# The low-rank norms of the attention's inputs, computed inside the input projection; the convolution's layer norm, inside the attention's projections

## The chip, the cores and the metric

The kernel is one program on one core of a Trainium2 chip. It runs two layers of a sequence mixer with an MLP behind each, and then one layer of another kind; all inputs and sums are float32. The metric is the device time of one execution in microseconds. The kernel before was timed in three runs, 3916.98 to 3918.47 us, with a median of 3918.4 us.

## The reference

There are 512 tokens of x and 256 of context, 768 together, each with 1024 features. What follows is the mixer of a layer, cut to what the change touches. In layer 0 all of it is computed for both kinds of token. In layer 1 the context takes part as keys, values and memory alone (`with_ctx` is false), so its convolution and its queries are not needed.

```python
DEPTH = 2;  CONV_DIM = 512;  CONV_K = 31;  Q_LORA = 768;  KV_LORA = 256;  QK_ROPE = 32

def layer_norm(x, g, b):
    mu = jnp.mean(x, -1, keepdims=True)
    var = jnp.mean(jnp.square(x - mu), -1, keepdims=True)
    return (x - mu) * lax.rsqrt(var + LN_EPS) * g + b

def rms_norm(x, g):
    return x * lax.rsqrt(jnp.mean(jnp.square(x), -1, keepdims=True) + LN_EPS) * g

def conformer_conv(a, w_dw, b_dw, g, b, w_pw):
    val, gate = jnp.split(a, 2, axis=-1)
    h = val * jax.nn.sigmoid(gate)
    h = depthwise_conv(h, w_dw, taps=CONV_K) + b_dw        # along the tokens, 15 before to 15 behind
    return jax.nn.silu(layer_norm(h, g, b)) @ w_pw

def mla_project(cq, ckv, kr, qn_g, w_uq, kvn_g, w_ukv, rope):
    q = rms_norm(cq, qn_g) @ w_uq                          # 8 heads of 64 + 32
    kv = rms_norm(ckv, kvn_g) @ w_ukv                      # 8 heads of 64 + 64
    ...                                                    # the 32s of q, and kr, are rotated

def token_mixer(u, uc, ...):
    a, qkv, o_pre, g_if, cq, ckv, kr, gates = jnp.split(u @ w_in + b_in, IN_SPLITS, axis=-1)
    y_conv = conformer_conv(a, ...)
    y_ml = mlstm_out(...)                                  # from qkv, o_pre, g_if
    o_x = attention over mla_project(cq, ckv, kr, ...)
    return gated_merge(gates, y_conv, y_ml, o_x @ w_mla_out, w_out, b_out)
```

## The kernel before, in words

Activations lie transposed: features on the 128 partitions, tokens along the free axis, 768 wide (512 and 256 for the two token kinds; 512 alone where layer 1 leaves the context out). A norm over features is therefore a sum over partitions. TensorE makes it with a matrix of ones, which also spreads the sum over all partitions.

**Weights.** They stream from HBM in groups of 128 output columns through a ring of 4 slots (`weight_ring`, queue of SP). The first three functions below that name runs and groups count a group as one slot. `plan_weights` fixes the order of the groups; in `project_stage` it is conv 8, qkv 12, o 4, cq 6, ckv 2, small 1: 33 groups in each layer. A group of such a product is split into a high part, made by ACT (L365, two groups ahead), and a low part, the subtraction on GpSimd (L373, `weights_low<-weight_ring,weights_high`).

**A group on TensorE** (`product`, L431): 8 feature tiles times the column parts, first the high weights by the high and the low activations (L448, L449), then, after a wait for the split, the low weights by the high activations (L454, 16 passes for a width of 768). Groups use two PSUM tiles in turn. A group waits (`tile_free`) until the tile's previous group has been taken out.

**The convolution.** Its input comes from pairs of groups: gates in the even ones, ACT makes their sigmoid; values in the odd ones, the vector engine multiplies them (L885, called the gating here, one instruction for each token kind) and then frees the odd tile. Four gatings stand first in the vector engine's program. Behind them come the four filters, each for 128 features: one instruction of tap 0 (L898) and a loop over the 30 other taps (L900 to L904), each tap a multiply-add over 512 tokens and one over 256, in layer 1 over 512 alone.

**The norm stage** (`norm_stage`, L984) stands between the projection and the attention, with a barrier of all engines on each side. It does the convolution's layer norm with its SiLU, and the two root-mean-square norms of ckv (2 tiles) and cq (6 tiles). Its sums are plain ones: L1008 for the mean, L1018 for the squares.

**The attention's beginning** (`attention_stage`, L1114). TensorE rotates the key's rope part (L1206), projects two rope tiles of the queries and four others (`queries_of`, L1198, 6 passes of 512 columns and in layer 0 6 of 256; here called the rope products and the query products 0 to 3), turns the rope tiles (L1211), then makes four products of keys (L1233, key products 0 to 3), and then the scores (L1249). These products read the normed cq and ckv. The convolution's result is not read before a later stage.

## Time and profile before

| | |
|---|---|
| median of 3 runs (lowest, highest) | 3918.4 us (3916.98, 3918.47) |
| the profiled execution: its own time | 3919.24 us |
| its span in the profile | 3917.4 us |
| TensorE matmul busy (PE) | 3503.9 us, 89% of the span |
| TensorE weight load (PEld) | 2727.3 us, 70% |
| vector engine (DVE) | 1735.0 us, 44% |
| ACT | 1088.0 us, 28% |
| GpSimd (POOL) | 1065.1 us, 27% |
| mean granted clock of TensorE | 0.929 of full speed |
| read from HBM | 265.56 MB |

The span is the time from the first to the last instruction of the core in one profiled execution; the execution's own time is a little longer. Busy time counts the time in which an engine works on an instruction; waits, branches and register instructions are not in it. The weight load runs beside the matmuls. The full speed of the clock column is 2.4 GHz. Such means cover the whole program; what a stage is worth has to be read in the stage itself.

### The profile page before, as it was taken

What the parts mean: (1) busy time and instruction counts of PE and PEld (TensorE: products, weight loads), DVE (VectorE), ACT (ScalarE), POOL (GpSimd) and SP (SyncE); (2) the same over time, 40 slices, a digit from 0 to 9 for tenths busy, and PEclk for the clock granted to TensorE, in tenths of its full rate; (3) what the DMA queues carried; (4) which work ended last, traced back from release to release, by engine and by line L of the source; (5) the groups of instructions that cost most, each with busy time, mean ns of one, the idle gap of its engine ahead of it and who ended that gap; (6) DMA issues with size and microseconds to landing.
All of it is one profiled execution on the core that took longest, in us unless ns stands there. A gap on an engine that the chain in (4) does not pass through costs nothing. (4 is left out here: it accounts for less than half of the span.)

```text
span 3917.4 us, 48973 instructions
## 1 busy us (share of the span) xinstructions
PE 3503.9 (89%) x18326; PEld 2727.3 (70%) x18326; DVE 1735.0 (44%) x2340; ACT 1088.0 (28%) x1540; POOL 1065.1 (27%) x491
## 2 busy tenths in 40 slices
PE   5899798879998799999797997799799979899998
PEld 4787466757776688888585566566577757678786
DVE  3592445450113522323486455412433348577625
ACT  1122243121112512221423231212432245333223
POOL 2532100111112222222333001222344423344442
PEclk7999898779999899999899997799899989899998
DMA  5222133012221122222122221232133322123232
GB/s 161 54 60 53 30 102 103 24 51 56 59 59 54 34 63 61 62 64 59 55 71 52 62 65 44 70 86 82 58 92 91 92 69 68 51 86 96 83 94 75
DMA packets 549094, 269.63 MB, mean 69 GB/s; under 512 B 55922, under 2 KB 547146, under 8 KB 548827
## 3 DMA queue, kind: packets, MB, share of 16 engines
q1 hardware_dynamic: 547330, 267.26, 24.2%
q8 instruction: 93, 1.52, 0.2%
q10 hardware_dynamic: 889, 0.30, 0.0%
q14 instruction: 46, 0.38, 0.0%
q0 software_dynamic: 736, 0.17, 0.0%
HBM read 265.56 MB, written 2.10 MB: 68 GB/s over the span
## 5 line engine op out<-in xcount | busy, mean ns | idle before, releaser
L373 POOL TENSOR_TENSOR weights_low<-weight_ring,weights_high 128x1024 fp32r<-128x1024 f32 x360 | 924.3, 2569 | 1782.8 <-ACT weights_high L365 1742.2
L365 ACT ACTIVATE weights_high<-weight_ring 128x1024 fp32r<-128x1024 f32 x360 | 380.3, 1059 | 1616.0 <-PE ps L454 1169.5
L448 PE MATMUL ps<-u_high,weights_high 128*128 128x512 f32 (+2 forms) x1440 | 533.2, 380 | 42.9 <-DVE u_low L751 35.1
L449 PE MATMUL ps<-u_low,weights_high 128*128 128x512 f32 (+2 forms) x1440 | 522.1, 373 | 0.0
L448 PEld LDWEIGHTS ps<-u_high,weights_high 128*128 128x128 f32 (+1 forms) x1440 | 275.8, 191 | 105.6 <-issue 29.6
L454 PE MATMUL ps<-u_high,weights_low 128*128 128x512 f32 (+2 forms) x1440 | 319.2, 369 | 15.8 <-POOL weights_low L373 15.8
L449 PEld LDWEIGHTS ps<-u_low,weights_high 128*128 128x128 f32 (+1 forms) x1440 | 276.9, 192 | 51.0 <-issue 3.7
L448 PE MATMUL ps<-mlp_u_high,weights_high 128*128 128x512 f32 (+1 forms) x768 | 268.4, 363 | 43.3 <-DVE mlp_u_low L751 42.3
L904 DVE SCALAR_TENSOR_TENSOR arena<-arena,vectors 128x512 f32<-128x512 f32 x360 | 293.2, 864 | 30.3 <-DVE arena L904 29.3
L454 PEld LDWEIGHTS ps<-u_high,weights_low 128*128 128x128 f32 (+1 forms) x1440 | 249.7, 190 | 61.6 <-POOL weights_low L373 16.0
L448 PE MATMUL ps<-hidden_high,weights_high 128*128 128x512 f32 (+1 forms) x768 | 263.8, 357 | 15.4 <-DVE hidden_low L2107 15.4
L449 PE MATMUL ps<-mlp_u_low,weights_high 128*128 128x512 f32 (+1 forms) x768 | 265.1, 360 | 0.0
L449 PE MATMUL ps<-hidden_low,weights_high 128*128 128x512 f32 (+1 forms) x768 | 261.5, 356 | 0.0
L2105 DVE TENSOR_TENSOR mlp_work<-mlp_work 128x768 f32<-128x768 f32 (+1 forms) x64 | 152.4, 2381 | 224.6 <-ACT mlp_work L2085 224.6
L1929 DVE TENSOR_TENSOR arena<-ps,arena 128x768 f32<-128x768 f32 (+3 forms) x48 | 39.6, 824 | 463.1 <-PE ps L467 463.1
L448 PE MATMUL ps<-merge_u_high,weights_high 128*128 128x512 f32 x576 | 212.0, 380 | 21.9 <-DVE merge_u_low L751 21.5
L2116 DVE SCALAR_TENSOR_TENSOR x_features<-ps,modulation,x_features 128x512 f32<-128x512 f32 x96 | 60.6, 659 | 355.0 <-PE ps L454 355.0
L467 PE MATMUL ps<-arena,weight_ring 128*128 128x512 f32 (+1 forms) x576 | 210.1, 521 | 0.0
L449 PE MATMUL ps<-merge_u_low,weights_high 128*128 128x512 f32 x576 | 201.8, 364 | 0.0
L448 PEld LDWEIGHTS ps<-mlp_u_high,weights_high 128*128 128x128 f32 x768 | 146.6, 191 | 72.9 <-issue 32.6
L448 PEld LDWEIGHTS ps<-hidden_high,weights_high 128*128 128x128 f32 x768 | 144.6, 188 | 40.5 <-DVE hidden_low L2107 17.9
L467 PEld LDWEIGHTS ps<-arena,weight_ring 128*128 128x128 f32 x576 | 108.5, 190 | 92.1 <-issue 86.1
(470 smaller groups left out, 5611.4 us busy)
## 6 DMA issues: line engine op xcount, KB each, us to landing
weight_ring<-in_w_in SPq DMA_DIRECT2D x262, 256.0 KB, 3.2
weight_ring<-in_w SPq DMA_DIRECT2D x256, 256.0 KB, 3.1
weight_ring<-in_w_mod SPq DMA_DIRECT2D x192, 256.0 KB, 4.0
weight_ring<-in_w_up SPq DMA_DIRECT2D x88, 256.0 KB, 3.1
weight_ring<-in_w_out SPq DMA_DIRECT2D x48, 256.0 KB, 3.1
weight_ring<-in_w_down SPq DMA_DIRECT2D x32, 256.0 KB, 3.2
weight_ring<-in_w_conv_out SPq DMA_DIRECT2D x32, 128.0 KB, 2.3
weight_ring<-in_w_mlstm_out SPq DMA_DIRECT2D x32, 128.0 KB, 2.3
```

Of the source, the lines that this page charges most:

```text
L365: act.activation(core.ring_high[:, split_slot(run, q), :], core.ring[:, slot, :], ACT.Copy).then_inc(core.high_ready.sem, 1)
L373: core.nc.gpsimd.tensor_tensor(core.ring_low[:, split_slot(run, q), :], core.ring[:, (run.first + q) % SLOTS, :], high.bitcast(F32), ALU.s ...
L448: pe.matmul(out[:, a:b], w_high[:, k, 0:m], high(k, a, b), start=(first and k == 0), stop=False, skip_group_check=True)
L449: pe.matmul(out[:, a:b], w_high[:, k, 0:m], low(k, a, b), start=False, stop=False, skip_group_check=True)
L454: mm = pe.matmul(out[:, a:b], w_low[:, k, 0:m], high(k, a, b), start=False, stop=(last and k == kts - 1), skip_group_check=True)
L467: mm = pe.matmul(out[:, a:b], w[:, k, :], rhs(k, a, b), start=(k == 0), stop=(k == kts - 1))
L904: nc.vector.scalar_tensor_tensor(conv[:, f, a:b], pads[:, f, bass.ds(t + at, b - a)], w_dw[:, bass.ds(t, 1), f], conv[:, f, a:b], ALU.mult ...
L1929: nc.vector.tensor_tensor(dst, gemm(core, 2 + f, w), sig[:, f, 0:w], ALU.mult).then_inc(multiplied.sem, 1)
L2105: nc.vector.tensor_tensor(squares[:, q % 2, 0:w], tmp[:, q % 2, 0:w], tmp[:, q % 2, 0:w], ALU.mult).then_inc(made.sem, 1)
L2116: ins = nc.vector.scalar_tensor_tensor(x, gemm(core, q % 2)[:, a:b], core.mod[l][:, 40 + q, j:j + 1], x, ALU.mult, ALU.add)
```

## The change

The groups of the projection are reordered: cq, ckv and small come right behind conv, and qkv and o behind these. The squares of cq and ckv are made by ACT as their groups come out, into room that qkv will fill later. TensorE sums them in a form of its own, `spread_sums`: four tiles at a time, each by a matrix of ones 32 columns wide, into its own 32 partitions of the output (behind cq's fifth group, and behind small). ACT copies the result, and `total_of_spread` (behind qkv's second group) adds up the four parts and spreads the total over all partitions. ACT makes the first guess of the reciprocal root (a logarithm, an exponential) behind qkv's third group. The vector engine refines it and scales cq and ckv (`scale_low_rank`, 16 instructions) between filters 2 and 3. ACT waits for that before qkv's ninth group, whose output lies where the intermediate values are.

On the vector engine filter 0 is cut into three loops of 10 taps, and the gatings 1 to 3 stand behind them.

The convolution's layer norm moves into the attention's projections. TensorE sums its four tiles before the first rope product, totals them behind it, and does the same for the squares behind query product 0 and query product 1. ACT makes the copies, squares, logarithm, exponential and the four SiLUs; the vector engine centers, refines and scales. Key product 0 now waits for the halved variance (`step` 2), since it takes the total's PSUM tile. ACT waits for the scaling before it copies the first keys, and GpSimd before its copies of the key's rope part. PSUM tiles are dealt out anew. The norm stage is no longer called. The diff, cut to what is spoken of:

```diff
         add(f"conv{l}", 8, paired(w_in, OFF_CONV + CONV_DIM, OFF_CONV))
-        add(f"qkv{l}", 12, plain(w_in, OFF_QKV))
-        add(f"o{l}", 4, plain(w_in, OFF_O))
         add(f"cq{l}", 6, plain(w_in, OFF_CQ))
...
         add(f"small{l}", 1, small)
+        add(f"qkv{l}", 12, plain(w_in, OFF_QKV))
+        add(f"o{l}", 4, plain(w_in, OFF_O))
...
+def spread_sums(core, pe, out, tiles, first, last):
...
+    for a, b in parts(T):
+        for g, tile in tiles:
+            if b <= tile.shape[1]:
+                mm = pe.matmul(out(g)[g * 32:(g + 1) * 32, a:b], core.ones[:, 0:32], tile[:, a:b], start=first(g), stop=last(g),
+                               skip_group_check=True)
+    return mm
...
+def total_of_spread(core, pe, out, partial, rows):
...
+    for a, b in parts(partial.shape[1]):
+        mm = pe.matmul(out[:, a:b], core.ones[rows, :], partial[rows, a:b], start=True, stop=True)
...
+                if (name, g) == ("cq", 4):
+                    pe.wait_ge(squared.sem, squared.at(4))
+                    spread_sums(core, pe, lambda j: gemm(core, 2), [(j, squares[:, j, 0:wx]) for j in range(4)], lambda j: True,
+                                lambda j: j >= 2).then_inc(half_summed.sem, 1)
+                elif name == "small":
+                    pe.wait_ge(squared.sem, squared.at(8))
+                    spread_sums(core, pe, lambda j: gemm(core, 2 + j // 2), [(j, squares[:, j, 0:(wx, T)[j // 2]]) for j in range(4)],
+                                lambda j: j >= 2, lambda j: True).then_inc(spread_summed.sem, 1)
+                elif (name, g) == ("qkv", 1):
+                    pe.wait_ge(spread_copied.sem, spread_copied.at(2))
+                    for j, (_, _, w, _, rows) in enumerate(norms):
+                        mm = total_of_spread(core, pe, gemm(core, 2 + j), partial[:, j, 0:w], rows)
+                    mm.then_inc(totals_ready.sem, 1)
...
                 elif name == "qkv":
+                    if g == 8:
+                        act.wait_ge(scaled.sem, scaled.at(8))
...
+                    if g >= 4:
+                        act.wait_ge(half_summed.sem, half_summed.at(1))
+                    act.activation(squares[:, g % 4, 0:w], src, ACT.Square, bias=col(core, f"b_cq{l}", g)).then_inc(squared.sem, 1)
                     act.activation(cq[:, g, 0:w], src, ACT.Identity, bias=col(core, f"b_cq{l}", g)).then_inc(free[f].sem, 1)
...
+                    act.activation(squares[:, 2 + g, 0:w], src, ACT.Square, bias=col(core, f"b_ckv{l}", g)).then_inc(squared.sem, 1)
...
+                elif (name, g) == ("qkv", 2):
+                    act.wait_ge(totals_ready.sem, totals_ready.at(1))
+                    for j, (_, tiles, w, _, _) in enumerate(norms):
+                        act.activation(rstd[:, j, 0:w], gemm(core, 2 + j, w), ACT.Ln, scale=1.0 / (32 * tiles * P),
+                                       bias=core.eps[:, 0:1]).then_inc(logged.sem, 1)
+                    for j, (_, _, w, _, _) in enumerate(norms):
+                        act.wait_ge(logged.sem, logged.at(j + 1))
+                        act.activation(rstd[:, j, 0:w], rstd[:, j, 0:w], ACT.Exp, scale=-0.5).then_inc(rstd_step.sem, 1)
...
-            for q in range(4):
+            def conv_input(q):
...
+            def scale_low_rank():
+                dve.wait_ge(rstd_step.sem, rstd_step.at(2))
+                for j, (_, tiles, w, _, _) in enumerate(norms):
...
+                for j, (z, tiles, w, gain, _) in enumerate(norms):
+                    dve.wait_ge(rstd_step.sem, rstd_step.at(9 + j))
+                    for k in range(tiles):
+                        nc.vector.scalar_tensor_tensor(z[:, k, 0:w], z[:, k, 0:w], col(core, gain, k), rstd[:, j, 0:w], ALU.mult,
+                                                       ALU.mult).then_inc(scaled.sem, 1)
...
+            def taps(f, lo, hi):
+                with dve.Fori(lo, hi) as t:
+                    for j, (a, b, at) in enumerate(spans):
...
+            conv_input(0)
             for f in range(4):
                 if f:
...
+                if f == 0:
+                    for q in range(1, 4):
+                        taps(0, 10 * q - 9, 10 * q + 1)
+                        conv_input(q)
+                else:
+                    taps(f, 1, CONV_K)
+                if f == 2:
+                    scale_low_rank()
...
+            def conv_sums(tiles):
+                spread_sums(core, pe, lambda g: gemm(core, 3), list(enumerate(tiles)), lambda g: True, lambda g: True)\
+                    .then_inc(c["spread_summed"].sem, 1)
+            def conv_totals(n):
+                pe.wait_ge(c["copied"].sem, c["copied"].at(n))
+                total_of_spread(core, pe, gemm(core, 3), partial[:, 0:wz], slice(0, P)).then_inc(c["totals_ready"].sem, 1)
+            conv_sums([z[:, f, 0:wz] for f in range(4)])
             pe.wait_ge(core.rope_weights.sem, core.rope_weights.at(64))
             queries_of("rope", 0, "qr0")
+            conv_totals(1)
             queries_of("rope", 1, "qr1")
             turn_queries(0)
+            pe.wait_ge(s["kr_rotated"].sem, s["kr_rotated"].at(1))
             queries_of("nope", 0, "qn0")
+            pe.wait_ge(c["squared"].sem, c["squared"].at(4))
+            conv_sums([squares[f][:, 0:wz] for f in range(4)])
...
+            pe.wait_ge(s["rope_step"].sem, s["rope_step"].at(1))
             queries_of("nope", 1, "qn1")
-            pe.wait_ge(s["rope_step"].sem, s["rope_step"].at(1))
+            conv_totals(2)
...
             queries_of("nope", 2, "qn2")
-            pe.wait_ge(s["rope_step"].sem, s["rope_step"].at(3))
+            pe.wait_ge(s["even_copied"].sem, s["even_copied"].at(1))
+            pe.wait_ge(s["odd_copied"].sem, s["odd_copied"].at(1))
             queries_of("nope", 3, "qn3")
...
+                if p:
+                    pe.wait_ge(s["even_copied"].sem, s["even_copied"].at(p + 3))
+                    pe.wait_ge(s["odd_copied"].sem, s["odd_copied"].at(p + 3))
+                else:
+                    pe.wait_ge(c["step"].sem, c["step"].at(2))
...
+                act.wait_ge(c["spread_summed"].sem, c["spread_summed"].at(n))
+                act.activation(partial[:, 0:wz], conv_total, ACT.Copy).then_inc(c["copied"].sem, 1)
+            spread_copy(1)
             raw_queries(0)
+            for f in range(4):
+                act.wait_ge(c["centered"].sem, c["centered"].at(f + 1))
+                act.activation(squares[f][:, 0:wz], z[:, f, 0:wz], ACT.Square).then_inc(c["squared"].sem, 1)
             raw_queries(1)
             for p in range(PAIRS):
+                if p == 1:
+                    spread_copy(2)
+                elif p == 2:
+                    act.wait_ge(c["totals_ready"].sem, c["totals_ready"].at(2))
+                    act.activation(mean[:, 0:wz], conv_total, ACT.Ln, scale=1.0 / (32 * CONV_DIM), bias=core.eps[:, 0:1])\
+                        .then_inc(c["logged"].sem, 1)
+                    act.wait_ge(c["logged"].sem, c["logged"].at(1))
+                    act.activation(mean[:, 0:wz], mean[:, 0:wz], ACT.Exp, scale=-0.5).then_inc(c["step"].sem, 1)
+                elif p == 3:
+                    for f in range(4):
+                        act.wait_ge(c["scaled"].sem, c["scaled"].at(f + 1))
+                        act.activation(z[:, f, 0:wz], z[:, f, 0:wz], ACT.Silu, scale=col(core, f"cn_g{l}", f), bias=col(core, f"cn_b{l}", f))
                 projected(act, f"qn{p}")
...
+                if p == 0:
+                    act.wait_ge(c["scaled"].sem, c["scaled"].at(4))
...
+            pool.wait_ge(c["scaled"].sem, c["scaled"].at(4))
...
+            dve.wait_ge(c["totals_ready"].sem, c["totals_ready"].at(1))
+            for f in range(4):
+                nc.vector.scalar_tensor_tensor(z[:, f, 0:wz], conv_total, -1.0 / (32 * CONV_DIM), z[:, f, 0:wz], ALU.mult,
...
+            step = c["step"]
+            dve.wait_ge(step.sem, step.at(1))
+            nc.vector.tensor_scalar(half[:, 0:wz], conv_total, -0.5 / (32 * CONV_DIM), -0.5 * LN_EPS, ALU.mult, ALU.add).then_inc(step.sem, 1)
...
-                    norm_stage(core, *norms)
                     attention_stage(core, l)
```

The tables of the program's order show two places. Names in capitals are instructions, ISA is a short one that carries a wait or a loop's counter, and [waits ...] names the semaphores that a row waits for.

The vector engine in layer 0, before: the last two gatings (L885), tap 0 of filter 0 (L898), and its loop.

```order
L885 SCALAR_TENSOR_TENSOR arena<-ps,vectors,arena 128x512 [waits conv_input_ready_27,gate_sigmoid_ready_26,weights_used_0]
L885 SCALAR_TENSOR_TENSOR arena<-ps,vectors,arena 128x256
L898 TENSOR_SCALAR arena<-arena,vectors 128x512 [waits conv_input_ready_27]
L898 TENSOR_SCALAR arena<-arena,vectors 128x256
L900 UNCONDITIONAL_BRANCH
L900 ISA
L904 ISA [waits conv_step_28]
L904 SCALAR_TENSOR_TENSOR arena<-arena,vectors 128x512
L904 ISA [waits conv_step_28]
L904 SCALAR_TENSOR_TENSOR arena<-arena,vectors 128x256
L900 REGISTER_ALU
L900 COMPARE_AND_BRANCH
```

The same place now: one gating (L940), tap 0 (L983), and the first ten taps (L969 to L973). The second gating follows, then the next ten, and so on.

```order
L940 SCALAR_TENSOR_TENSOR arena<-ps,vectors,arena 128x512 [waits gate_sigmoid_ready_26,weights_used_0,pads_clear_29]
L940 SCALAR_TENSOR_TENSOR arena<-ps,vectors,arena 128x256
L983 TENSOR_SCALAR arena<-arena,vectors 128x512 [waits conv_input_ready_27]
L983 TENSOR_SCALAR arena<-arena,vectors 128x256
L969 UNCONDITIONAL_BRANCH
L969 ISA
L973 ISA [waits conv_step_28]
L973 SCALAR_TENSOR_TENSOR arena<-arena,vectors 128x512
L973 ISA [waits conv_step_28]
L973 SCALAR_TENSOR_TENSOR arena<-arena,vectors 128x256
L969 REGISTER_ALU
L969 COMPARE_AND_BRANCH
```

The three gatings have moved from in front of the filter to places between its taps, and the wait for the gates' sigmoid with them. The body of the loop is the same four instructions. In filter 1 the loop's body is another one. Before:

```order
L904 ISA [waits conv_step_28]
L904 REGISTER_ALU
L904 SCALAR_TENSOR_TENSOR arena<-arena,vectors 128x512
L903 REGISTER_ALU
L904 ISA [waits conv_step_28]
L904 SCALAR_TENSOR_TENSOR arena<-arena,vectors 128x256
```

And now, the body of filter 1's loop:

```order
L973 ISA [waits conv_step_28]
L973 REGISTER_ALU
L973 SCALAR_TENSOR_TENSOR arena<-arena,vectors 128x512
L972 REGISTER_ALU
L973 ISA [waits conv_step_28]
L973 SCALAR_TENSOR_TENSOR arena<-arena,vectors 128x256
```

Both have a REGISTER_ALU between the ISA and the first tap, and one between the taps. Filter 0's loop has neither, before and now.

TensorE at the end of layer 0's norm stage, before: the last sum of squares, the barrier, the key's rotation and the first rope products.

```order
L1018 MATMUL ps<-heads,ones 128x512 [waits norm2_squared_44]
L1018 MATMUL ps<-heads,ones 128x256
L1000 UNCONDITIONAL_BRANCH
L1189 UNCONDITIONAL_BRANCH [waits barrier_Pool_Activation_PE_DVE_SP_release]
L1206 MATMUL ps<-arena,rope 32x512 [waits rope_loaded_7]
L1198 MATMUL ps<-arena,weight_ring 128x512 [waits weights_landed1,rope_weights_landed_8]
L1198 MATMUL ps<-arena,weight_ring 128x512 x5
L1198 MATMUL ps<-arena,weight_ring 128x256 x6
L1198 MATMUL ps<-arena,weight_ring 128x512 [waits weights_landed2]
```

Now, behind the projection's last low pass: the barrier, the key's rotation, the spread sum (L784, by a matrix of ones 32 columns wide), the first rope product (L1293), the total (L792), the second.

```order
L830 UNCONDITIONAL_BRANCH
L1284 UNCONDITIONAL_BRANCH [waits barrier_Pool_Activation_PE_DVE_SP_release]
L1301 MATMUL ps<-arena,rope 32x512 [waits rope_loaded_7]
L784 MATMUL ps<-arena,ones 32x512 x4
L784 MATMUL ps<-arena,ones 32x256 x4
L1293 MATMUL ps<-arena,weight_ring 128x512 [waits weights_landed1,rope_weights_landed_8]
L1293 MATMUL ps<-arena,weight_ring 128x512 x5
L1293 MATMUL ps<-arena,weight_ring 128x256 x6
L792 MATMUL ps<-heads,ones 128x512 [waits at_conv_copied_62]
L792 MATMUL ps<-heads,ones 128x256
L1293 MATMUL ps<-arena,weight_ring 128x512 [waits weights_landed2]
```

The norm stage's sums of full width are gone, and with them one of the two barriers. Between the key's rotation and the rope products stand only sums that have no wait of their own or wait for ACT's copy.

## Rows read from the trace of the kernel before

**Rows 1.** Windows of both norm stages; each engine's busy us (instructions), granted clock, DMA.
```profile
379.40:430.00 50.60, 21.14 (x64) 11.88 (x64) 27.66 (x24) 23.44 (x27) 9.23 (x4) 0.76 0.02 4
2122.00:2160.00 38.00, 14.95 (x36) 5.86 (x35) 20.73 (x24) 18.45 (x27) 7.07 (x4) 0.78 0.00 0
```

**Rows 2.** Timeline of TensorE, layer 0; start us, us, line, operation [idle before <-releaser].
```profile
374.34 2.96 PE L454 MATMUL ps<-u_high,weights_low 128*96 128x512 f32 x16
379.44 5.40 PE L1008 MATMUL ps<-arena,ones 128*128 128x512 f32 x16 [2.14 <-PEq L807]
...
430.34 1.88 PE L1206 MATMUL ps<-arena,rope 32*32 32x512 f32 x2 [26.99 <-PEq L1000]
432.15 18.07 PE L1198 MATMUL ps<-arena,weight_ring 128*128 128x512 f32 x48
```

**Rows 3.** The same of TensorE, layer 1.
```profile
2116.14 2.96 PE L454 MATMUL ps<-u_high,weights_low 128*96 128x512 f32 x16
...
2161.65 13.41 PE L1198 MATMUL ps<-arena,weight_ring 128*128 128x512 f32 x24
```

**Rows 4.** Timeline of the vector engine, layer 0's convolution.
```profile
153.24 31.83 DVE L904 SCALAR_TENSOR_TENSOR arena<-arena,vectors 128x512 f32<-128x512 f32 x60
185.10 4.83 DVE L898 TENSOR_SCALAR arena<-arena,vectors 128x512 f32<-128x512 f32 x2
189.85 42.61 DVE L904 SCALAR_TENSOR_TENSOR arena<-arena,vectors 128x512 f32<-128x512 f32 x60
```

**Rows 5.** Timeline of GpSimd, the same stretch.
```profile
158.74 28.53 POOL L373 TENSOR_TENSOR weights_low<-weight_ring,weights_high 128x1024 fp32r<-128x1024 f32 x1 [6.03 <-ACT weights_high L365]
```

**Rows 6.** Timeline of TensorE, the same stretch.
```profile
187.32 4.79 PE L454 MATMUL ps<-u_high,weights_low 128*128 128x512 f32 x16 [15.79 <-POOL weights_low L373]
```

**Rows 7.** Timeline of ACT, ends of three groups in layer 0's projection.
```profile
157.60 1.06 ACT L365 ACTIVATE weights_high<-weight_ring 128x1024 fp32r<-128x1024 f32 x1 [7.36 <-PE ps L454]
166.02 1.06 ACT L365 ACTIVATE weights_high<-weight_ring 128x1024 fp32r<-128x1024 f32 x1 [6.57 <-PE ps L454]
192.20 1.06 ACT L365 ACTIVATE weights_high<-weight_ring 128x1024 fp32r<-128x1024 f32 x1 [24.33 <-PE ps L454]
```

**Rows 8.** Timeline of the vector engine, layer 1: first gating, first filter, second filter's start.
```profile
1915.07 0.75 DVE L885 SCALAR_TENSOR_TENSOR arena<-ps,vectors,arena 128x512 f32<-128x512 f32 x1 [9.29 <-PE ps L454]
...
1949.38 0.55 DVE L898 TENSOR_SCALAR arena<-arena,vectors 128x512 f32<-128x512 f32 x1
1950.23 2.51 DVE L904 SCALAR_TENSOR_TENSOR arena<-arena,vectors 128x512 f32<-128x512 f32 x1 [0.30 <-DVE arena L898]
1953.01 0.75 DVE L904 SCALAR_TENSOR_TENSOR arena<-arena,vectors 128x512 f32<-128x512 f32 x1 [0.27 <-DVE arena L904]
...
1993.21 0.55 DVE L898 TENSOR_SCALAR arena<-arena,vectors 128x512 f32<-128x512 f32 x1
```

**Rows 9.** Timeline of ACT, layer 1, the end of group 8.
```profile
1954.11 1.06 ACT L365 ACTIVATE weights_high<-weight_ring 128x1024 fp32r<-128x1024 f32 x1 [4.51 <-PE ps L454]
```

**Rows 10.** Timeline of TensorE in an MLP stage, round a short wait.
```profile
2956.37 0.39 PE L448 MATMUL ps<-hidden_high,weights_high 128*128 128x512 f32 x1
2956.60 0.39 PE L449 MATMUL ps<-hidden_low,weights_high 128*128 128x512 f32 x1
2959.34 0.79 PE L448 MATMUL ps<-hidden_high,weights_high 128*128 128x512 f32 x1 [2.35 <-DVE hidden_low L2107]
2960.36 3.09 PE L454 MATMUL ps<-hidden_high,weights_low 128*128 128x512 f32 x8
```

**Rows 11.** Timeline of TensorE in layer 0's attention.
```profile
459.51 23.38 PE L1198 MATMUL ps<-arena,weight_ring 128*128 128x512 f32 x72
...
508.95 1.08 PE L637 MATMUL ps<-weight_ring,conditions 128*32 128x128 f32 x32
```

**Rows 12.** Timeline of ACT in layer 0's norm stage, a table load.
```profile
404.31 1.28 ACT L1042 ACT_TABLE_LOAD   x1
```

**Rows 13.** Timeline of the vector engine in layer 0's norm stage.
```profile
424.36 5.66 DVE L1086 SCALAR_TENSOR_TENSOR arena<-arena,vectors,heads 128x768 f32<-128x768 f32 x6
```

76 lines of the change are left out of this document (54 added, 22 removed).

## The prediction

> **What bounds the kernel now.** I read the two windows that hold the norm stages first, then TensorE's rows on both sides of them, then the vector and GpSimd rows of the convolution, for that loop is cut up too. In the windows [rows 1] the reader is to see that TensorE works for 21.14 of 50.60 us in layer 0's norm stage and for 14.95 of 38.00 us in layer 1's, at a granted clock of 0.76 and 0.78 of 2.4 GHz, while before and behind it is the engine that everything waits for. Its rows [rows 2, 3] give the borders: in layer 0 the last projection product ends at 374.34 + 2.96 = 377.30, the second rope product at 432.15 + 18.07 = 450.22: 72.9 us. In layer 1 the borders are 2116.14 + 2.96 = 2119.10 and 2161.65 + 13.41 = 2175.06: 56.0 us. All of this is on the path.
>
> The second place is inside layer 0's projection [rows 4 to 7]. Filter 0's 60 tap instructions run 31.83 us without a gap; the GpSimd subtraction that makes the low half of a weight group starts at 158.74 and takes 28.53 us, until the vector engine comes to filter 1's first instruction at 185.10. TensorE waits 15.79 us for it and then runs 16 low passes in 4.79 us where they take 2.96 elsewhere [rows 2]. From group to group ACT's rows are 8.42 us apart (157.60, 166.02) and here 26.18 (166.02, 192.20). So the starved subtraction costs 17.8 us. Filter 1's 60 taps take 42.61 us, and TensorE does not stall there: the subtraction gets in between. In the order of instructions filter 0's loop of layer 0 is the one without a REGISTER_ALU between its taps, before and after.
>
> **The change, part by part.**
>
> 1. *Filter 0 cut in three (layer 0).* A chunk is 20 instructions, 31.83 / 3 = 10.6 us, inside two groups, 16.8 us, with 1.3 us of gating and one wait for a subtraction of about 2.5 us (it holds up a tap that is 0.75 us long until 2.51, [rows 8]): it ends before the next odd group does, so TensorE waits for no gating. A subtraction asked for 1.1 us behind a group's end (158.74 against 157.60) is due 8.42 + 8.42 − 2.96 = 13.9 us behind that end, where the low passes after the next begin, 12.8 us after it was asked for. The worst it can meet is a whole chunk and its own length, 13.1 us. So the stall goes: −17.8. Bounds: nothing gained (it is starved as before) to −17.8.
>
> 2. *The same cut in layer 1.* Here a group lasts 5.58 us, and the gating now stands between taps. Counted from 0, group 5 cannot start before gating 1, group 7 before gating 2, group 9 before gating 3, for they use the same PSUM tile. One filter takes 1993.21 − 1949.38 = 43.8 us [rows 8]: 30 taps of 0.75 + 0.25, and 7 of them long (2.51) because a subtraction holds the vector engine up. Gating 0 is at 1915.07; behind it come 0.9 us to the filter, 43.8 us, and 3 more gatings of 1.1 us: 1963.1 before group 9 may start. In the old trace group 8 ends at 1954.1 [rows 9]. TensorE is held back 9.1 us, in three waits of about 1.5, 5 and 3 us. After a wait of 2.35 us [rows 10] ten passes run from 2959.34 to 2963.45, 4.1 us, where passes 0.23 us apart (2956.37, 2956.60) and the last one's tail take 2.5: 1.6 us lost at the lower clock. Only the last wait's loss counts, the vector engine sets the time until then: with 0.2 us for each of the waits to be seen, +1.8. Together +10.9. Bounds: 0 (if the subtractions cost the taps nothing: 7 × 1.76 = 12.3 us less) to +16 (each of the three waits with its own 1.7 us at the lower clock, and two more subtractions met).
>
> 3. *Sums in the projection.* A float32 pass of 512 columns takes 0.43 us and one of 256 takes 0.215: 72 passes in 23.38 us [rows 11]. A plain sum of four 768-wide tiles is 4 × 1.29 = 5.16 us. The new ones use 32 columns of the array for each tile. The trace has no such product 512 wide; the nearest is L637 with 128 columns, 32 passes in 1.08 us [rows 11], 0.034 each against 0.107 at the rate above: 3.2 times as fast. So a sum costs 1.6 us (between 1.29, a quarter, and 5.16, no overlap at all), in layer 1 1.1 or 1.3. Two sums in each layer: +3.2 and +2.4. Two totals: +2.6 and +2.15. What they wait for (squares, the copy) is made by ACT in the group before, where it idles over 6 of 8.4 us [rows 7]. ACT's extra work at the third qkv group (two table loads of 1.28 us [rows 12], two logarithms and two exponentials of 0.9, about 6 us) is over before its next weight part is due in either layer. The vector engine's 16 instructions for scaling, at 5.66 / 6 = 0.94 to 0.96 us [rows 13], about 16 us, stand between filters 2 and 3, and ACT waits for them only at the ninth qkv group. Counted back from the projection's end (377.3 − 17.8 + 5.8), the third qkv group has 13 groups behind it and ends near 256, so the rstd is there near 263 and the values are scaled near 285; the ninth qkv group ends near 306. In layer 1 filter 2 ends near 2053 (1963 + 2 × 45), the scaling near 2070, the ninth qkv group near 2087. The last filter ends well before TensorE does: nothing on the path.
>
> 4. *The norm stages go.* Behind the last projection product now come one barrier instead of two, about 1.4 us (2.1 before, 377.30 to 379.44, in which ACT had two evictions and now has one), the key rotation 0.9 (1.88 at the lower clock), one sum, a rope product of 7.74, a total of 1.29, a rope product of 7.74: 20.7 us in place of 72.9: −52.2. The 2.1 us gap before L1008 did not lower the clock, so I count full speed. Layer 1: 1.4 + 0.9 + 1.1 + 5.15 + 0.86 + 5.15 = 14.6 in place of 56.0: −41.4. What is late next: layer 0's weights for these products land 3 us after issue and are asked for three groups earlier.
>
> 5. *Added behind that.* One more sum and one more total: +2.9 in layer 0, +1.9 in layer 1. The new wait is that of key product 0 for the halved variance, with everything of the attention queued behind it. With t the end of query product 1: total at t + 1.3, ACT's table load, Ln, table load, Exp to t + 6, vector engine to t + 7. Key product 0 comes at t + 1.3 + 2 × 7.74 = t + 16.8 (layer 1: t + 11.2 against t + 5.8). Key product 1 also needs ACT's copy of query product 3, which now stands behind four SiLUs: t + 18 against t + 19.4, in layer 1 t + 13.6 against t + 13.8. Costed at nothing; in layer 1 a microsecond more on ACT would show at once. GpSimd's key copies now wait for the scaling, but end near t + 20.5, seven microseconds before the first score.
>
> Sum, layer 0: −17.8 + 5.8 − 52.2 + 2.9 = −61.3. Layer 1: +10.9 + 4.6 − 41.4 + 1.9 = −24.0. Together −85.3. The profiled execution took 3919.2 us (span 3917.4), so 3834; it is 0.8 us above the median of the runs, which is less than I can resolve.
>
> The Trainium skill, page "TensorEngine Tiling (Array Packing)", section "Theoretical Speedup", allows up to four times for 32 columns. With its factor, an estimate, all eight sums would cost 2.2 us less than with the 3.2 of the row, and the result would be 3832. Its section "Tiling Modes" also says that changing the tiling mode drains the engine, which speaks against sums strewn among full-width products; no row here prices that.
>
> **Rivals.**
>
> *Sums without overlap.* If four column groups 512 wide run one after the other, the eight sums cost 35.2 us instead of 11.0: 3858. For it: no wide one has been seen. Against it: L637 reads four different moving operands too.
>
> *No wait in layer 1.* If TensorE is not held by the gating, part 2 gives 0 and the time is 3823. For it: each microsecond that TensorE stands still takes subtractions away from the vector engine. Against it: with no long tap at all the chain ends 12.3 us earlier, at 1950.8 where 1954.1 is needed, so only one or two of the seven subtractions may cost it anything.
>
> *Starvation moves.* The scaling has 8 instructions without a wait between them, 7.8 us, and with those in front 14 or so; if they shut the subtraction out as filter 0 does, it comes up to 3.4 us late, with 2 us of clock, and in the chunks of filter 0 some may come late as well: up to 12 us, 3846. The Trainium skill, page "SBUF — State Buffer", section "SBUF: two separate sides", has the port between the two engines as a lock held for one whole instruction, so that the other would get in after each tap. The trace agrees for the single long tap (2.51 us) and disagrees for the 28.53 us one; by the page this rival would not exist.
>
> *Slower.* The one mechanism that reaches the other side is this starvation in all filters. If the register instruction between the taps no longer lets the subtraction in, filters 1 to 3 of layer 0 cost 17.8 us each, 53, and the four of layer 1, each some 22.5 us of taps against a reserve of 5 to 10 us, about 11 each: 45. Then 3834 + 98 = 3932. It decides from about 87 us of new stalls. Against it: those loops keep their instructions.
>
> **How the numbers follow.** Forecast 0.62; sums without overlap 0.11; no wait in layer 1 0.10; starvation moves 0.14, with anything else late in the attention; slower 0.02; and 0.01 that gains and losses cancel. The forecast case alone spans 3826 to 3843. The range reaches into the cases on both sides: 3820 to 3859. A measurement of this kernel tells about 0.2% (8 us) from no change. All cases but the last two are faster by more: 0.97; same 0.01; slower 0.02.
>
> **What would show it.** Right: no row of GpSimd's subtraction over about 14 us in layer 0; TensorE waiting near groups 5, 7 and 9 of layer 1 for the gating, 9 us together; the new 32-column sums at about 1.6 us for 16 passes; under 2 us between the last projection product and the attention's first, at the full clock; 12 passes of width 512 and 12 of 256 in 7.74 us right behind. Wrong: those sums near 5 us; a wait at key product 0 or 1; a wait of a low product for GpSimd; a lower clock at the start of the attention.

## The result and the profile after

The changed kernel takes 3831.1 us (median of 4 runs, 3829.5 to 3831.8), the one before 3917.7 us (4 runs, 3915.2 to 3918.5): a ratio of 0.9779, with a 95% interval of 0.9763 to 0.9796. That is 86.6 us less; forecast were 85.3, and 3834. All medians here are of executions at the usual clock: a single one, of the kernel with layer 0's filter 0 whole, took 4350 us at a granted clock of 0.76 and is left out.

| | before | changed |
|---|---|---|
| span of the profiled execution | 3917.4 us | 3827.6 us |
| TensorE busy | 3503.9 us, 89% | 3477.7 us, 91% |
| vector engine | 1735.0 us | 1743.1 us |
| ACT | 1088.0 us | 1099.6 us |
| GpSimd | 1065.1 us | 1036.7 us |
| mean granted clock | 0.929 | 0.938 |

Busy time hardly moved: TensorE worked 26 us less and waited 64 us less. Where it did so is read by stretches of the span. A window of the changed kernel is set from the first product of a projection to the end of its last, and from there to key product 0. The columns are the stretch and its length, busy us of TensorE, weight load, vector engine, ACT and GpSimd with their instructions, the granted clock, and the DMA. First the changed kernel, layer 0's two stretches and layer 1's:

```profile
68.09:365.61 297.52, 291.47 (x1624) 249.06 (x1624) 210.42 (x288) 80.06 (x91) 105.48 (x36) 0.97 0.22 55
365.61:421.88 56.27, 54.84 (x191) 30.64 (x192) 25.46 (x38) 19.30 (x21) 3.69 (x5) 1.00 0.22 50
1829.62:2074.32 244.70, 229.09 (x1082) 183.39 (x1082) 175.32 (x160) 74.13 (x91) 90.37 (x36) 0.95 0.26 68
2074.32:2114.97 40.65, 39.22 (x99) 16.32 (x100) 19.84 (x30) 15.20 (x21) 0.86 (x2) 0.96 0.30 68
```

Then the stretches of the kernel before (its first projection runs from 67.31 to 377.30, 309.99 us):

```profile
377.30:482.74 105.44, 73.54 (x215) 41.22 (x216) 42.20 (x50) 29.27 (x34) 15.48 (x12) 0.85 0.12 27
1889.00:2119.10 230.10, 221.43 (x1056) 181.44 (x1056) 157.40 (x144) 59.72 (x73) 91.57 (x36) 0.96 0.28 72
2119.10:2197.22 78.12, 52.93 (x115) 21.98 (x116) 32.83 (x42) 24.00 (x34) 13.32 (x12) 0.85 0.15 36
```

| stretch | before | changed | difference | forecast |
|---|---|---|---|---|
| ahead of layer 0's projection | 67.3 | 68.1 | +0.8 | 0 |
| layer 0's projection | 310.0 | 297.5 | −12.5 | −12.0 |
| from there to key product 0 | 105.4 | 56.3 | −49.2 | −49.3 |
| up to layer 1's projection | 1406.3 | 1407.7 | +1.5 | 0 |
| layer 1's projection | 230.1 | 244.7 | +14.6 | +15.5 |
| from there to key product 0 | 78.1 | 40.7 | −37.5 | −39.5 |
| from there to the end | 1720.2 | 1712.6 | −7.6 | 0 |
| span | 3917.4 | 3827.6 | −89.8 | −85.3 |

The reader is to see that in both norm stretches TensorE is now busy but for the 1.4 us of one barrier (54.84 of 56.27, 39.22 of 40.65), and that layer 1 pays 14.6 us in its projection for the 37.5 it saves.

No edit of TensorE's work lies in the last line of the table: it makes the same passes there, before and now. The differences come in steps of about 1 us up and down, more than half of them in layer 1's memory stage. The same stretch took 1713.5 to 1720.2 us in the five kernels of this document that keep the old order of groups, the one before among them, and 1711.9 to 1716.1 us in the nine that have the new one. The two groups overlap, but lie about 4 us apart in the mean, and no run shows why. The four stretches that the change touches come to −84.6 us, the two profiled executions differ by 89.8, and the medians by 86.6; the medians are the better number for the whole.

The lines that answer to [rows 2] are TensorE's, from the end of layer 0's projection into the attention:

```profile
362.64 2.97 PE L454 MATMUL ps<-u_high,weights_low 128*128 128x512 f32 x16
367.04 1.01 PE L1301 MATMUL ps<-arena,rope 32*32 32x512 f32 x2 [1.43 <-PEq L830]
367.98 1.50 PE L784 MATMUL ps<-arena,ones 128*32 128x512 f32 x16
369.41 8.01 PE L1293 MATMUL ps<-arena,weight_ring 128*128 128x512 f32 x24
377.25 1.45 PE L792 MATMUL ps<-heads,ones 128*128 128x512 f32 x4
378.55 7.90 PE L1293 MATMUL ps<-arena,weight_ring 128*128 128x512 f32 x24
```

One gap of 1.43 us stands where 2.14 and 26.99 us stood in [rows 2]. The spread sum (L784) occupies TensorE from 367.98 to 369.41, the total (L792) from 377.25 to 378.55, and the first rope product follows at the full clock (1.00 over the whole stretch in this execution).

To [rows 5] answer the subtractions of GpSimd while filter 0 runs and while cq and ckv are scaled, and to [rows 4] the first two pieces of the filter on the vector engine:

```profile
108.15 7.43 POOL L373 TENSOR_TENSOR weights_low<-weight_ring,weights_high 128x1024 fp32r<-128x1024 f32 x1 [6.02 <-ACT weights_high L365]
...
124.99 6.71 POOL L373 TENSOR_TENSOR weights_low<-weight_ring,weights_high 128x1024 fp32r<-128x1024 f32 x1 [6.02 <-ACT weights_high L365]
...
265.80 3.17 POOL L373 TENSOR_TENSOR weights_low<-weight_ring,weights_high 128x1024 fp32r<-128x1024 f32 x1 [6.03 <-ACT weights_high L365]
```

```profile
102.66 10.66 DVE L973 SCALAR_TENSOR_TENSOR arena<-arena,vectors 128x512 f32<-128x512 f32 x20
115.37 1.15 DVE L940 SCALAR_TENSOR_TENSOR arena<-ps,vectors,arena 128x512 f32<-128x512 f32 x2 [2.05 <-PE ps L454]
116.99 12.44 DVE L973 SCALAR_TENSOR_TENSOR arena<-arena,vectors 128x512 f32<-128x512 f32 x20 [0.47 <-DVE arena L940]
```

A tap is two instructions here, one for each token kind, so a piece of ten taps is the row with x20. It runs 10.66 us without a break, and the subtraction that is asked for inside it ends 2.26 us behind it (108.15 + 7.43 = 115.58; 102.66 + 10.66 = 113.32). The 28.53 us one is gone. No low pass of TensorE (L454) waits for a subtraction in this projection.

Layer 1, TensorE: its three waits for the gating (released by the vector engine's queue at L944), and the beginning of the attention:

```profile
1874.00 0.47 PE L448 MATMUL ps<-u_high,weights_high 128*128 128x512 f32 x1 [1.46 <-DVEq L944]
...
1890.42 0.76 PE L448 MATMUL ps<-u_high,weights_high 128*128 128x512 f32 x1 [4.98 <-DVEq L944]
...
1903.58 0.47 PE L448 MATMUL ps<-u_high,weights_high 128*128 128x512 f32 x1 [0.49 <-DVEq L944]
...
2075.75 1.01 PE L1301 MATMUL ps<-arena,rope 32*32 32x512 f32 x2 [1.43 <-PEq L830]
2076.69 1.14 PE L784 MATMUL ps<-arena,ones 128*32 128x512 f32 x8
2077.76 7.00 PE L1293 MATMUL ps<-arena,weight_ring 128*128 128x512 f32 x12
2084.59 1.02 PE L792 MATMUL ps<-heads,ones 128*128 128x512 f32 x2
```

The waits are 1.46, 4.98 and 0.49 us, 6.9 together. At 2077.76 twelve passes take until 2084.59, 6.8 us at a granted clock of 0.77, where the next twelve take 5.2 at 1.00.

### The profile page after: what moved, and what is told of

The parts are those of the page before. It is cut to its first block and busy times, and to the rows that moved or that the text cites. A ratio compares the mean times of both kernels' runs of the same rounds, so it can differ in the third digit from the quotient of the medians.

```text
span 3827.6 us, 49027 instructions
## 1 busy us (share of the span) xinstructions
PE 3477.7 (91%) x18352; PEld 2709.0 (71%) x18352; DVE 1743.1 (46%) x2348; ACT 1099.6 (29%) x1550; POOL 1036.7 (27%) x483
## 5 line engine op out<-in xcount | busy, mean ns | idle before, releaser
L373 POOL TENSOR_TENSOR weights_low<-weight_ring,weights_high 128x1024 fp32r<-128x1024 f32 x360 | 912.3, 2536 | 1803.4 <-ACT weights_high L365 1762.7
L448 PE MATMUL ps<-u_high,weights_high 128*128 128x512 f32 (+1 forms) x1440 | 533.8, 380 | 49.8 <-DVE u_low L751 35.3
L449 PE MATMUL ps<-u_low,weights_high 128*128 128x512 f32 (+1 forms) x1440 | 521.9, 373 | 0.0
L448 PEld LDWEIGHTS ps<-u_high,weights_high 128*128 128x128 f32 x1440 | 275.8, 192 | 116.3 <-issue 37.4
L454 PE MATMUL ps<-u_high,weights_low 128*128 128x512 f32 (+1 forms) x1440 | 316.7, 367 | 0.0
L973 DVE SCALAR_TENSOR_TENSOR arena<-arena,vectors 128x512 f32<-128x512 f32 x360 | 298.9, 880 | 35.4 <-DVE arena L973 31.9
L449 PEld LDWEIGHTS ps<-u_low,weights_high 128*128 128x128 f32 x1440 | 276.8, 192 | 50.5 <-issue 3.4
L454 PEld LDWEIGHTS ps<-u_high,weights_low 128*128 128x128 f32 x1440 | 247.5, 188 | 45.4
```

The source lines that it names most:

```text
L373: core.nc.gpsimd.tensor_tensor(core.ring_low[:, split_slot(run, q), :], core.ring[:, (run.first + q) % SLOTS, :], high.bitcast(F32), ALU.s ...
L448: pe.matmul(out[:, a:b], w_high[:, k, 0:m], high(k, a, b), start=(first and k == 0), stop=False, skip_group_check=True)
L449: pe.matmul(out[:, a:b], w_high[:, k, 0:m], low(k, a, b), start=False, stop=False, skip_group_check=True)
L454: mm = pe.matmul(out[:, a:b], w_low[:, k, 0:m], high(k, a, b), start=False, stop=(last and k == kts - 1), skip_group_check=True)
L973: nc.vector.scalar_tensor_tensor(conv[:, f, a:b], pads[:, f, bass.ds(t + at, b - a)], w_dw[:, bass.ds(t, 1), f], conv[:, f, a:b], ALU.mult ...
```

## The experiments

All are timed against the kernel before on the same chip, where its median was between 3914.0 and 3917.7 us. Where one is compared with the changed kernel, it is by the medians: 3831.1 us for the changed kernel. Such a difference can be off by these 4 us; the lengths of the stretches say more. Pieces are counted in taps, rows in instructions.

| kernel | median us | ratio to before, 95% interval |
|---|---|---|
| changed | 3831.1 | 0.9779, 0.9763 to 0.9796 |
| layer 0's filter 0 whole | 3847.2 | 0.9826, 0.9806 to 0.9845 |
| layer 1's filter 0 whole | 3827.3 | 0.9772, 0.9756 to 0.9788 |
| before, a register instruction between the taps | 3916.6 | 1.000, 0.9991 to 1.001 |
| before, one ahead of the first tap too | 3900.5 | 0.9958, 0.9942 to 0.9975 |
| before, filter 1 first | 3922.8 (one run) | |
| changed, no register instruction between the taps | 3830.9 | 0.9781, 0.9765 to 0.9797 |
| changed, first piece of 20 taps in layer 0 | 3837.3 | 0.9801, 0.9785 to 0.9818 |
| changed, pieces of 6 taps in layer 1 | 3820.5 | 0.9755, 0.9741 to 0.9768 |
| layer 0 whole and counted from 0, pieces of 6 in layer 1 | 3821.5 | 0.9755, 0.9742 to 0.9769 |
| changed, sums in one column group | 3845.7 | 0.9820, 0.9807 to 0.9833 |
| low-rank norms alone | 3872.4 | 0.9890, 0.9875 to 0.9905 |
| convolution's norm alone | 3894.1 | 0.9941, 0.9926 to 0.9956 |

### Filter 0 of layer 0 whole

```diff
-            conv_input(0)
+            whole = l == 0
+            for q in range(4 if whole else 1):
+                conv_input(q)
...
-                if f == 0:
+                if f == 0 and not whole:
```

> The changed kernel, but in layer 0 the four gatings stand in front of filter 0 again and its 30 taps are one loop; layer 1 keeps the three pieces. Theory (the cut into pieces is what removes the starved subtraction): one subtraction of GpSimd of about 28 us returns, TensorE waits about 15.8 us for it, and the time rises by 17.8 us to about 3849. Rival (the gain in the projection has another cause, such as the new order of the groups): within 3 us of the changed kernel's 3831.

Measured 3847.2 us, 16.1 more than the changed kernel; the projection takes 315.33 us instead of 297.52, 17.8 more. GpSimd's and TensorE's lines are those of before again:

```profile
158.83 28.54 POOL L373 TENSOR_TENSOR weights_low<-weight_ring,weights_high 128x1024 fp32r<-128x1024 f32 x1 [6.03 <-ACT weights_high L365]
```

```profile
187.41 4.53 PE L454 MATMUL ps<-u_high,weights_low 128*128 128x512 f32 x16 [15.79 <-POOL weights_low L373]
```

So the 17.8 us is what the cut into pieces gives, with the gatings between them, and not the new order of the groups: the stall is the same in either order.

### What lets the subtraction in

Four kernels ask why filter 0 shuts GpSimd out and filters 1 to 3 don't. The first raises the counter in layer 0:

```diff
+    more = 8 if l == 0 else 0
...
+            if more:
+                dve.sem_inc(conv_step.sem, more)
...
-                        dve.wait_ge(conv_step.sem, t * n + (conv_step.at(CONV_K * f * n) - n + j + 1))
+                        dve.wait_ge(conv_step.sem, t * n + (conv_step.at(CONV_K * f * n) + more - n + j + 1))
```

> The kernel before, in which in layer 0 the taps' counter is raised by 8 ahead of filter 0, so that the wait value has to be computed: filter 0's loop gets one register instruction between its two taps, and the others keep theirs. Nothing else changes. If the register instruction is what lets GpSimd in: the 28.53 us subtraction shrinks to about 2.5 us, and the time falls by 17.8 us to about 3900. If something else starves it (the vector engine's load as such, or the phase): it stays over 20 us, and the time at 3918.

Measured 3916.6 us: no change. The register instruction between the taps is not it:

```profile
160.40 28.53 POOL L373 TENSOR_TENSOR weights_low<-weight_ring,weights_high 128x1024 fp32r<-128x1024 f32 x1 [6.03 <-ACT weights_high L365]
```

The second is the opposite, on the changed kernel: each filter has a counter of its own.

```diff
+    steps_of = [conv_step] + [core.flag(f"conv_step{f}") for f in (1, 2, 3)]
...
-                        dve.wait_ge(conv_step.sem, t * n + (conv_step.at(CONV_K * f * n) - n + j + 1))
+                        dve.wait_ge(steps_of[f].sem, t * n + (steps_of[f].at(0) - n + j + 1))
```

> The changed kernel with a counter of its own for each filter, so that in layer 0 filters 1 to 3 lose the register instruction between their two taps (one ahead of the first tap stays); layer 1 keeps its loops. If the instruction between the taps is what lets GpSimd in: subtractions of up to 30 us in filters 1 to 3 and about 17.8 us of stall for each, 53 us together, so about 3884. If the one ahead of the first tap is enough: 3831.

Measured 3830.9 us. Filters 1 to 3 of layer 0 do without the instruction between the taps and keep the one ahead of the first, and no subtraction of layer 0 is longer than in the changed kernel. The third counts from 0, in the kernel before:

```diff
-                with dve.Fori(1, CONV_K) as t:
+                one = 1 if f == 0 and both else 0
+                with dve.Fori(1 - one, CONV_K - one) as t:
...
-                        nc.vector.scalar_tensor_tensor(conv[:, f, a:b], pads[:, f, bass.ds(t + at, b - a)],
-                                                       w_dw[:, bass.ds(t, 1), f], conv[:, f, a:b], ALU.mult,
+                        nc.vector.scalar_tensor_tensor(conv[:, f, a:b], pads[:, f, bass.ds(t + (at + one), b - a)],
+                                                       w_dw[:, bass.ds(t + one, 1), f], conv[:, f, a:b], ALU.mult,
```

> The kernel before, in which the loop of filter 0 in layer 0 counts from 0 to 29 instead of from 1 to 30 and adds the one where it is used. Its body thereby gets a register instruction directly ahead of its first tap, as filters 1 to 3 have, beside one between the taps. The run with one between the taps alone changed nothing. If the one ahead of the first tap is what lets GpSimd in: no subtraction over 5 us, TensorE's wait of 15.8 us goes, and the time falls by 17.8 us to about 3898. If filter 0 starves GpSimd by its place in time or by the addresses of its data: 3916, with a subtraction of over 28 us.

Measured 3900.5 us, a ratio of 0.9958 (0.9942 to 0.9975). The projection of layer 0 takes 292.28 us, 17.7 less than before, and no low pass waits for a subtraction. The whole gains less than the 17.8 forecast, 13.5 us by the medians on that chip (3914.0 before) and 16 by the ratio. One place shows it: in the profiled execution the stretch behind, up to key product 0, took 109.2 us and not 105.4, at a granted clock of 0.83 and not 0.85. Filter 0 and filter 1 on the vector engine, and GpSimd's first two subtractions beside filter 0:

```profile
155.44 42.60 DVE L905 SCALAR_TENSOR_TENSOR arena<-arena,vectors 128x512 f32<-128x512 f32 x60
198.87 42.60 DVE L905 SCALAR_TENSOR_TENSOR arena<-arena,vectors 128x512 f32<-128x512 f32 x60
```

```profile
160.89 2.86 POOL L373 TENSOR_TENSOR weights_low<-weight_ring,weights_high 128x1024 fp32r<-128x1024 f32 x1 [6.03 <-ACT weights_high L365]
169.31 2.94 POOL L373 TENSOR_TENSOR weights_low<-weight_ring,weights_high 128x1024 fp32r<-128x1024 f32 x1 [5.56 <-ACT weights_high L365]
```

Same taps, same data, same addresses, same place in time; the loop's body has a register instruction ahead of the 512-wide tap, filter 0's loop lasts 42.60 us as filter 1's does, and these subtractions take 2.9 us. The fourth changes the place in time:

```diff
-            for f in range(4):
-                if f:
+            for i, f in enumerate((1, 0, 2, 3) if both else range(4)):
+                if i:
```

> The kernel before, in which layer 0 does filter 1 ahead of filter 0. Filter 1's loop, now the first, keeps its register instruction ahead of the first tap (there is none between the taps); filter 0's, now the second, has one between the taps and none ahead of the first. If the place in time decides: the long subtraction stays where it is, near 159 us. If the loop's own instructions or filter 0's addresses decide: it moves to the second loop, near 200 us. The time is about 3916 either way.

Filter 1's output lies where filter 0's input was, so in this one filter 0 reads other numbers; the work is the same. The first loop is now filter 1's and the second filter 0's:

```profile
153.67 42.60 DVE L904 SCALAR_TENSOR_TENSOR arena<-arena,vectors 128x512 f32<-128x512 f32 x60
...
197.10 31.84 DVE L904 SCALAR_TENSOR_TENSOR arena<-arena,vectors 128x512 f32<-128x512 f32 x60
```

```profile
201.22 29.92 POOL L373 TENSOR_TENSOR weights_low<-weight_ring,weights_high 128x1024 fp32r<-128x1024 f32 x1 [5.89 <-ACT weights_high L365]
```

```profile
231.19 5.09 PE L454 MATMUL ps<-u_high,weights_low 128*128 128x512 f32 x16 [17.18 <-POOL weights_low L373]
```

The starvation moved with filter 0's loop, to 201 us, and TensorE waits 17.18 us for it there. The one execution took 3922.8 us where 3916 was expected; 1.4 us of that are the longer wait, the rest isn't explained. Filter 1's loop, now first, has the register instruction ahead of the first tap alone, and it lets the subtractions in. What decides between these loops is thus their own sequence, and of the two register instructions the one ahead of the first tap. Why that one works isn't settled: it costs no time that the rows show (60 tap instructions take 31.8 us without it and 42.6 with it, which leaves 10.8 for the five subtractions that fall into a loop, one in 8.4 us).

### How long a piece may be

```diff
+                    ends = (1, 21, 26, 31) if both else (1, 11, 21, 31)
                     for q in range(1, 4):
-                        taps(0, 10 * q - 9, 10 * q + 1)
+                        taps(0, ends[q - 1], ends[q])
```

> The changed kernel, but in layer 0 filter 0 is cut into pieces of 20, 5 and 5 taps; layer 1 keeps 10, 10, 10. By the rule that a subtraction caught in a piece ends 2.3 us behind it: the first piece runs from 102.7 to 124.0, the subtraction asked for at 108.2 ends at 126.3, and the low passes that need it are due at 120.8, so TensorE waits about 5.5 us once, with some lower clock: about 3837. If pieces of any length did: 3831.

Measured 3837.3 us. The first piece on the vector engine, GpSimd and TensorE:

```profile
103.52 21.25 DVE L973 SCALAR_TENSOR_TENSOR arena<-arena,vectors 128x512 f32<-128x512 f32 x40
```

```profile
109.01 17.97 POOL L373 TENSOR_TENSOR weights_low<-weight_ring,weights_high 128x1024 fp32r<-128x1024 f32 x1 [6.02 <-ACT weights_high L365]
```

```profile
127.03 4.45 PE L454 MATMUL ps<-u_high,weights_low 128*128 128x512 f32 x16 [5.23 <-POOL weights_low L373]
```

The subtraction ends at 126.98, 2.2 us behind the piece (103.52 + 21.25 = 124.77), and TensorE waits 5.23 us. The rule of the forecast holds: a subtraction caught in a piece is late when the piece's rest and 2.2 to 2.3 us reach past the next group's low passes.

### Layer 1: whole, and in pieces of 6

The first has the edit of the first experiment with `whole = l == 1`.

> The changed kernel, but in layer 1 the four gatings stand in front of filter 0 and its taps are one loop; layer 0 keeps the pieces. Rival A (the pieces in layer 1 only cost): TensorE's three waits of 1.46, 4.98 and 0.49 us for the gating go, with about 1.5 us of lower clock: about 3823. My theory: all filters begin some 32 us later, the scaling of cq and ckv ends near 2041 instead of 2009, ACT cannot take out the ninth qkv group before that, TensorE stands still about 15 us at the eleventh, and the last filter ends about 3 us behind TensorE: 8.4 won, about 19 lost, so about 3842.

Measured 3827.3 us: my theory named the right wait and put far too high a price on it. TensorE's wait for ACT (L900, its copy of the ninth qkv group out of PSUM), and the last of the scaling that ACT waits for:

```profile
2033.49 0.76 PE L448 MATMUL ps<-u_high,weights_high 128*128 128x512 f32 x1 [5.40 <-ACT arena L900]
```

```profile
2026.44 5.91 DVE L963 SCALAR_TENSOR_TENSOR arena<-arena,vectors 128x512 f32<-128x512 f32 x8
```

The wait is 5.40 us and not 15: the scaling ends at 2032.3 and not at 2041, because filters 0 to 2 took 44.0, 42.1 and 40.1 us (forecast 45 each) and the scaling 13.9 (forecast 16). Fewer subtractions met filters 1 and 2, since beside 768-wide groups they come only every 8.4 us. The last filter ends ahead of TensorE. The projection takes 243.4 us against 244.7 in pieces of ten: in layer 1 the two are worth the same within what can be told.

The second has pieces shorter than the 11.2 us of two groups:

```diff
+                    size = 6 if l == 1 else 10
                     for q in range(1, 4):
-                        taps(0, 10 * q - 9, 10 * q + 1)
+                        taps(0, size * (q - 1) + 1, size * q + 1)
                         conv_input(q)
+                    if 3 * size + 1 < CONV_K:
+                        taps(0, 3 * size + 1, CONV_K)
```

> The changed kernel, but in layer 1 filter 0 is cut into pieces of 6, 6, 6 and 12 taps with the gatings behind the first three; layer 0 keeps pieces of 10. A piece of 6 with two subtractions takes about 9.8 us, less than the 11.2 us of two groups of width 512. Theory: the three waits of TensorE for the gating (6.9 us) go with about 1.5 us of lower clock: 8.4 us less, about 3823. Rival (what TensorE no longer waits comes back as subtractions that meet more taps, or at the first product of the attention): within 3 us of 3831.

Measured 3820.5 us, 10.6 less than the changed kernel. Gatings 1 to 3 on the vector engine now wait for TensorE's group or come just behind it, and not the other way round; below them the windows of layer 0's stretch up to key product 0, of layer 1's projection, and of layer 1's stretch up to key product 0:

```profile
1868.52 0.75 DVE L940 SCALAR_TENSOR_TENSOR arena<-ps,vectors,arena 128x512 f32<-128x512 f32 x1
1879.67 0.75 DVE L940 SCALAR_TENSOR_TENSOR arena<-ps,vectors,arena 128x512 f32<-128x512 f32 x1 [0.18 <-PE ps L454]
1890.83 0.75 DVE L940 SCALAR_TENSOR_TENSOR arena<-ps,vectors,arena 128x512 f32<-128x512 f32 x1 [0.21 <-PE ps L454]
```

```profile
366.13:424.04 57.91, 56.48 (x191) 31.11 (x191) 25.48 (x38) 19.31 (x21) 3.67 (x5) 0.97 0.21 48
1831.32:2066.79 235.47, 226.80 (x1082) 182.75 (x1082) 178.48 (x160) 74.15 (x91) 92.09 (x36) 0.96 0.27 70
2066.79:2105.79 39.00, 37.57 (x98) 15.67 (x99) 19.85 (x30) 15.20 (x21) 0.85 (x2) 1.00 0.31 71
```

The projection takes 235.5 us (244.7), 9.2 less. Of this 6.9 were waits; 1.4 more lay in the group behind the longest wait, which in the changed kernel took 6.9 us instead of 5.6 and began at a granted clock of 0.50. The beginning of layer 1's attention runs at the full clock, 1.65 us less, but that isn't the pieces' doing: in layer 0, where this kernel is as changed, the same passage took 57.91 us at a mean clock of 0.97, 1.64 more than the 56.27 of the changed kernel.

The last kernel has these pieces of 6 in layer 1 (`not both`), leaves out those in layer 0, and counts its filter 0 from 0, with the one added as above:

```diff
-            conv_input(0)
+            for q in range(4 if both else 1):
+                conv_input(q)
...
-                if f == 0:
+                if f == 0 and not both:
...
-                with dve.Fori(lo, hi) as t:
+                one = 1 if f == 0 and both else 0
+                with dve.Fori(lo - one, hi - one) as t:
```

> The version that the runs point to: in layer 0 the gatings first and filter 0's loop whole, counted from 0 so that its body has the register instruction ahead of the first tap; in layer 1 pieces of 6, 6, 6 and 12 taps. All else as changed. In layer 0 filter 2 then ends near 281, the scaling near 300, and the ninth qkv group near 306, so nothing waits. If the pieces in layer 0 mattered for the starvation alone: as with pieces of ten in layer 0, 3820.5, within 3 us. If the scaling or the last filter comes late: 5 to 15 us more.

Measured 3821.5 us, and layer 0's projection takes 298.6 us (297.5 in the changed kernel). In layer 0 the pieces served only to keep the starvation short; one register instruction does it as well. One thing differs: in the refinement ahead of the scaling a subtraction now takes 7.05 us, where the changed kernel had 3.17 at most. Nothing waited for it.

```profile
283.74 7.05 POOL L373 TENSOR_TENSOR weights_low<-weight_ring,weights_high 128x1024 fp32r<-128x1024 f32 x1 [5.62 <-ACT weights_high L365]
```

### Sums in one column group

```diff
-                spread_sums(core, pe, lambda g: gemm(core, 3), list(enumerate(tiles)), lambda g: True, lambda g: True)\
-                    .then_inc(c["spread_summed"].sem, 1)
+                for a, b in parts(wz):
+                    for g, tile in enumerate(tiles):
+                        mm = pe.matmul(gemm(core, 3)[0:32, a:b], core.ones[:, 0:32], tile[:, a:b], start=(g == 0), stop=(g == 3))
+                mm.then_inc(c["spread_summed"].sem, 1)
```

> The changed kernel, but the attention's four spread sums (two in each layer) put their four tiles one after the other into the same 32 columns of the array and the same 32 partitions of the output; the total then reads 32 partitions. As many passes of the same size. If the four column groups work side by side: 16 passes take 5.16 us instead of 1.43 in layer 0, 8 take 3.44 instead of 1.0 in layer 1, together 12.4 us, so about 3843. If passes of 32 columns are cheap by themselves: no change, 3831.

Measured 3845.7 us, 14.6 more. The first sum of layer 0 and both of layer 1:

```profile
368.94 7.04 PE L1311 MATMUL ps<-arena,ones 128*32 128x512 f32 x16
...
2088.17 3.62 PE L1311 MATMUL ps<-arena,ones 128*32 128x512 f32 x8
2109.47 3.62 PE L1311 MATMUL ps<-heads,ones 128*32 128x512 f32 x8
```

In layer 1 a sum takes 3.6 us against 1.06 to 1.14, at the same width and with the same number of passes. In layer 0 the first takes 7.04 at a granted clock of 0.75, where 5.16 was forecast: most of the 2 us above the forecast. The rival "sums without overlap" is refuted: passes in four different column groups run side by side.

### The parts alone

The first of two kernels has the changed order and projection, the attention of before, and a norm stage in between:

```diff
                     core.free = space(inner, f"heads{l}", FREE)
+                    core.norm_scratch = core.free
+                    norms = [Norm(conv_view(core), conv_view(core), 4, w, lambda f: col(core, f"cn_g{l}", f),
+                                  lambda f: col(core, f"cn_b{l}", f), func=ACT.Silu, on_pool=True)]
+                    norm_stage(core, *norms)
                     attention_stage(core, l)
```

> One part of the change alone: order of the groups, pieces of filter 0 and low-rank norms as changed; the convolution's norm in a norm stage of its own as before, and the attention as before. By the chain in the rows, a stage with this norm alone lasts about 29 us in layer 0 in place of 50.6 and about 26 in layer 1: 28 and 25 us more than the changed kernel, about 3884. If the norm stage's time went with the number of its instructions (the convolution's norm has about a third of them), it would be nearer 3865.

Measured 3872.4 us. TensorE in layer 0: the sum for the mean, the sum of squares, and the key's rotation behind 14.60 us of waiting; and the windows from the projections' ends to key product 0:

```profile
367.14 5.40 PE L1097 MATMUL ps<-arena,ones 128*128 128x512 f32 x16 [1.43 <-PEq L830]
375.31 5.43 PE L1107 MATMUL ps<-heads,ones 128*128 128x512 f32 x16 [2.77 <-ACT heads L1124]
395.33 1.03 PE L1295 MATMUL ps<-arena,rope 32*32 32x512 f32 x1 [14.60 <-PEq L1089]
```

```profile
365.71:447.71 82.00, 63.20 (x183) 35.14 (x184) 21.92 (x34) 19.02 (x21) 13.34 (x12) 0.90 0.15 34
2098.31:2156.55 58.24, 43.74 (x94) 18.07 (x95) 17.36 (x26) 15.37 (x21) 11.18 (x12) 0.88 0.20 48
```

The second has the order and the projection of before, the changed attention, and the norm stage with the other two norms:

```diff
+                    norms = []
+                    for at, n, width, gain in ((A_CKV, 2, T, "kvn_g"), (A_CQ, 6, w, "qn_g")):
+                        norms.append(Norm(view(core, at, n), view(core, at, n), n, width,
+                                          lambda f, gain=gain: col(core, f"{gain}{l}", f), center=False))
+                    norm_stage(core, *norms)
                     attention_stage(core, l)
```

> The other part alone: projection and order of the groups as before, a norm stage with the two low-rank norms alone, and the attention with the convolution's norm in it. Layer 0: the stall of 17.8 us is back, the sums in the projection (5.8 us) are gone, and a norm stage of about 33 us and its barrier stand in front: 47 us more than the changed kernel. Layer 1: 14.6 us less in the projection, about 30 for the stage: 16 more. Together about 3894. The two parts alone would then win 34 and 24 of the 87 us, since either leaves most of a chain of waits in place; if the parts simply added up, this kernel would stand at 3865 when the other stands at 3884.

Measured 3894.1 us. The same windows:

```profile
377.54:469.08 91.54, 69.24 (x224) 37.55 (x224) 40.64 (x54) 32.64 (x37) 3.68 (x5) 0.89 0.13 31
2105.80:2177.52 71.72, 52.30 (x118) 21.20 (x119) 32.36 (x46) 27.03 (x37) 0.85 (x2) 0.83 0.17 39
```

Against the changed kernel the first is 25.7 us longer in layer 0, as expected (28), and 17.6 in layer 1, where I expected 25: there the chain of one norm at a width of 512 is shorter than I read it. The second is 35.3 and 31.1 us longer, and has the projections of before. With the projections' share it is 47.3 and 16.7 us above the changed kernel, as expected (47 and 16).

The two do not add up. Of the 86.6 us the low-rank norms alone win about 44 and the convolution's norm alone about 22. In the norm stretch of layer 0, 105.4 us long, they take off 23.4 and 13.9, both together 49.2; in layer 1 19.9 and 6.4 of 78.1, together 37.5. The forecast had 34 and 24 us for the parts, and 3884 us for the first kernel; the 3872.4 us measured lie nearer to the 3865 of its rival, by which the stage's time goes with the number of its instructions. The rival in its plain form would have the parts add up, which they don't, but the price of a chain with one norm was put too high, and how it divides between waits and work isn't shown. What the rows show is this: as long as one norm is left in the stage, its chain of sum, logarithm, exponential, refinement and scaling has to be waited out, with two barriers and TensorE at the lower clock for a part of it (0.83 to 0.90 in the mean of these windows).

## Why the prediction was right

*1, the pieces in layer 0 (−17.8).* Right in size and in cause: 17.8 us by the first experiment. The rule for the worst case (the rest of the piece and then the subtraction, which ends 2.2 to 2.3 us behind it) is in the rows and held at twice the length. What the prediction put down only as a correlation, that filter 0's loop has no register instruction between its taps, was half right: such a loop is the one that starves, but what it lacks is the register instruction ahead of the first tap.

*2, the pieces in layer 1 (+10.9).* The mechanism, the groups and the first two waits were right (1.46 and 4.98 us against 1.5 and 5); the third was 0.49 and not 3. The pieces of six give back 9.2 us in the projection, which is its price. The sum was 1.7 us too high, by that third wait. A likely reason, which no run isolates, is that the subtractions stop while TensorE stands still: between 1889.0 and 1898.8 none ran, which the rival "no wait in layer 1" had named. The upper bound of this part, +16, comes to 17.7 by its own terms (9.1, three times 1.7, twice 1.76).

*3, sums in the projection (+5.8, +4.6).* A spread sum takes 1.43 us in layer 0 (forecast 1.6), and 1.0 to 1.1 in layer 1 at a width of 512 (forecast 1.1), a total of width 768 1.30. What all this adds to a projection is 5.2 us in layer 0 (297.52 against 292.28 in the kernel before that counts from 0) and 5.4 in layer 1 (235.47 with pieces of six against 230.10 before). A plain sum of 5.16 us is 3.6 times the 1.43. The Trainium skill, page "TensorEngine Tiling (Array Packing)", section "Theoretical Speedup", allows four, and the forecast took 3.2 from an old row. Its section "Tiling Modes" has the engine drained when the mode changes; here a sum takes, with the change to narrow columns and back, 0.14 us more than a quarter of a plain one (1.43 against 1.29), so two drains cost no more than that.

*4, the norm stages go (−52.2, −41.4), and 5, what is added (+2.9, +1.9).* Together −49.2 and −37.5 measured, −49.3 and −39.5 forecast. In layer 0 every term held in this execution. The full clock there was in part luck: of the seven kernels that have this stretch unaltered, the changed one and the one with layer 0's filter 0 whole took 56.27 us, the five others 57.9. In layer 1 the first rope product lost 1.7 us at a granted clock of 0.77, where I had counted the full clock (a lower clock there was among the signs of being wrong); the wait in front of it is the same 1.43 us as in layer 0, so the row of before from which I took this did not carry over. Nothing waited at key product 0 or 1, in layer 1 the vector engine's step was done 5.7 us ahead of the first (2109.26 against 2114.97), and the last copies 1.7 us ahead of the second.

*What was luck in the number.* The four stretches that the change touches came to −84.6 us against −85.3: 0.5 more won than forecast in layer 0's projection, 0.9 less lost in layer 1's, 2.1 less won in the two stretches behind them. These errors are small, and they partly cancel. The 2 us between 84.6 and the 86.6 of the medians belong to no term.

*The rivals.* Sums without overlap would have cost 24 us; the one-column kernel shows what that looks like. Starvation moved, 12 us: in the changed kernel's scaling a subtraction takes 3.17 us and not 10, so there it gets in between 768-wide instructions. That the mechanism exists all the same shows in the last kernel of the pieces, where the same instructions, met at another moment, held one up for 7.05 us; that is 5.8 us less than the 12.8 it had. Slower, by starvation in all filters: refuted by the changed kernel, and by the one without the instruction between the taps. The danger behind it is real as far as the one ahead of the first tap goes: the loop that lacks it took its stall, 17.2 us, with it to the second place. Filters 1 to 3 without it were not run. On the lock between the two engines the Trainium skill, page "SBUF — State Buffer", section "SBUF: two separate sides", says that it is held for one whole instruction. The rows agree where a register instruction comes ahead of the tap (2.86 us). Where none does, the subtraction waits through some 50 tap instructions (28.53 us), which a lock held for one instruction does not explain.

## What to carry to other kernels

A norm as a stage of its own costs its chain of waits and two barriers as well as its work; put its sums behind products that run anyway, and take all norms out of the stage. Here the convolution's norm left alone in it cost 25.7 of 49.2 us in layer 0 and 17.6 of 37.5 in layer 1, the two low-rank norms 35.3 and 31.1. Before a long run of vector instructions is put beside work of GpSimd, look at how long one of GpSimd's rows lasts within it. Put work that frees a tile behind pieces shorter than the time between two such frees, in each layer by its own group time: pieces of ten taps fit the 768-wide groups and held up the 512-wide ones.

## What was not expected of the hardware

In this loop of two vector instructions on the same data, a register instruction ahead of the longer one decides whether a GpSimd instruction beside it takes 2.9 us or waits for the rest of the loop (28.5 us); one ahead of the shorter changes nothing, and the rows show no time lost by either. Outside the loops it isn't the instructions alone: in the refinement and scaling, with 768-wide instructions, a subtraction took 3.17 us in the changed kernel and 7.05 in another with the same ones.

The same passage, 1.43 us of barrier and two short groups of narrow passes, lowered TensorE's clock in some executions and not in others, without a change in it. In layer 0 it did so in five of seven kernels (57.9 us against 56.3 for the stretch), in layer 1 in four of seven (40.7 against 39.0), and the changed kernel had one of each: 1.00 in layer 0, 0.77 for 6.8 us in layer 1. So a difference of 1.6 us in such a stretch says nothing of an edit; what decides isn't settled here.
